# A decoder step on one core: memory K/V projection first, the SSD scan spread among dense tiles, page units and self heads moved behind it

## The chip, the core and the metric

The kernel runs on one core of one Trainium2 chip. The metric is device time in microseconds (us) of one execution. The core has TensorE (matmuls and transposes, results in PSUM), VectorE (DVE in the rows), ScalarE (ACT), GpSimd (POOL) and SyncE (SP, here only an issuer of DMAs). Each engine takes its instructions in the order in which the program lists them, and engines wait for one another by semaphores.

## What is computed

One layer of a hybrid decoder in float32, for a prompt of 256 tokens and 8 samples of 4 tokens with paged caches (288 token columns in all), and a final norm:

```python
proj = rmsnorm(h) @ w_in                       # z, xbc, dt_raw, q, k, v
y_ssd = ssd_branch(z, xbc, dt_raw, ...)        # causal conv, scan in chunks of 128, gate silu(z), norm
y_att = moba_attention(q, k_all, v_all, ...)   # samples: 1024 cached tokens; block top-k, relative bias
h = h + concat([y_ssd, y_att]) @ w_out
h = h + cross_attend(rmsnorm(h), mem_k, mem_v) # 4 heads over 256 memory tokens
h = h + square(relu(rmsnorm(h) @ w_up)) @ w_down
y = rmsnorm(h)
# prompt: mem_k, mem_v = split(rmsnorm(mem) @ w_ca_kv); samples: cached mem_k, mem_v
```

Outputs are also the new k, v, memory k and v, conv states and SSD states (8 heads of 64 for attention, 16 heads of 64 x 128 for the states).

## The kernel before

Activations lie transposed, channels on partitions and the 288 tokens as columns. A dense product is a series of blocks of 256 output columns (a pair of tiles of 128). Its weights (1 MB for 8 k-tiles) stand in one of four slots of `wring`; SyncE loads a block once an earlier one's products are done. A tile is 8 matmuls of 288 columns, each of which the trace shows as two passes, in PSUM bank 0 or 1; VectorE scales the result by `rstd` and writes it out (`tile_out`).

The kinds of tiles are q and k (`qk`, 4 pairs), `v` (2), `z` (4), `x` (6, each followed by the causal conv on VectorE), memory k and v (`m`, 4), `out` (4, with 8 k-tiles from z and 4 from attention), `caq` (2) and `cao` (4). All other results of TensorE (transposes, small products) go through "turns": PSUM banks 2, 3, 6 in rotation, emptied by ScalarE and VectorE alternately (`turn`, `bank`, `leave`).

The cached keys and values of the samples come as 16 *page units* of 2 MB, (K or V, group of four samples, quarter of the cache), eight pages of 256 KB each. `kvring` holds two units. `load_unit` on SyncE waits until the unit two before is used up (`slot_free`: for K its last transposes, for V its products), then loops over eight pages: it reads the page number from `pages` and issues one DMA. A K unit on TensorE is 32 transposes, evicted into `KT_`, and 64 narrow score products (`k_unit`); a V unit is 8 products in two passes (`v_unit`). After the four K units of a group, `own` and `self_bounds` form the scores' maxima and the block choice on VectorE; `probs` transposes the probabilities; `pvend` takes the result after the four V units. The prompt's own attention is eight *self heads* (`head`): scores, bias from DRAM, exp, norm, transposes, values. The units ST, MK and MV (SSD states, memory K and V of the samples) use the same ring with plain DMAs.

The order of everything is written out by hand in `make_plan`; each engine walks through the same list `SEQ` and does its part. Before the change: q/k pairs, with `early` (transposes and norm of the memory prompt, conv history) after the first; K units and pairs (qk, v, m) alternating; V units, self heads and pairs (x, z) alternating; then `ssd`, in one piece: a meeting of all engines, the scan over chunks 0, 1 and the samples' chunk, the state updates; then `out`, `caq`, cross attention, `cao`, MLP.

The SSD part works per chunk: tokens transposed (`xtok`, `btok`), sums of dt, `segments` (exponent matrices of 4 heads, 512 columns), `mix` on VectorE, `outputs`, gate by silu(z), chunk state; for the samples 16 state reads and 16 updates. `sq`, `acc` and the ss products form the sums of squares of a norm: ScalarE squares, GpSimd adds, TensorE sums over partitions, ScalarE takes the root, VectorE the reciprocal (`invert`).

Of the kernel before, what the change touches and what calls it, by code (L numbers as in the profile page):

```python
# [10 lines left out]
ALU = mybir.AluOpType  # L11
# [4 lines left out]
P = 128  # L16
# [91 lines left out]

def make_plan():
    seq = []  # L110

    def pair(kind, n, chunks):
        seq.append(("pair", kind, n, chunks))
# [7 lines left out]
    pair("qk", 0, 1)  # L121
    item("ss", 0)
    item("early")
    pair("qk", 1, 1)
    unit("K", 0, 0)
    pair("qk", 2, 1)
    unit("K", 0, 1)
    pair("qk", 3, 1)
    unit("K", 0, 2)
    pair("v", 0, 1)  # L130
    unit("K", 0, 3)
    item("own", 0)
    pair("v", 1, 1)
    unit("K", 1, 0)
    item("kvtok")
    item("ss", 1)
    pair("m", 0, 1)
    unit("K", 1, 1)
    item("probs", 0)
    pair("m", 1, 1)  # L140
    unit("K", 1, 2)
    pair("m", 2, 1)
    unit("K", 1, 3)
    item("own", 1)
    pair("m", 3, 1)
    item("mtok")
    item("heads_in", "self")
    pair("x", 0, 1)
    unit("V", 0, 0)
    item("head", "self", 0)  # L150
    pair("x", 1, 1)
    unit("V", 0, 1)
    item("head", "self", 1)
    pair("x", 2, 1)
    unit("V", 0, 2)
    item("head", "self", 2)
    pair("x", 3, 1)
    unit("V", 0, 3)
    item("pvend", 0)
    item("probs", 1)  # L160
    item("head", "self", 3)
    pair("x", 4, 1)
    unit("V", 1, 0)
    item("head", "self", 4)
    pair("x", 5, 1)
    item("dt")
    unit("V", 1, 1)
    pair("z", 0, 1)
    item("head", "self", 5)
    pair("z", 1, 1)  # L170
    unit("V", 1, 2)
    item("silu_x")
    item("head", "self", 6)
    pair("z", 2, 1)
    pair("z", 3, 1)
    unit("V", 1, 3)
    item("pvend", 1)
    item("head", "self", 7)
    item("heads_end", "self")
    item("ssd")  # L180
    item("ss", 2)
    for n in range(4):
        pair("out", n, 2)
    pair("caq", 0, 1)
    item("ss", 3)
    pair("caq", 1, 1)
# [15 lines left out]
    for n in range(4):  # L202
        pair("cao", n, 1)
    item("ss", 4)
    return seq


SEQ = make_plan()
BLOCK, TILE, UNIT, TURN = {}, {}, {}, {}
USED = {}  # L210
for s in SEQ:
    if s[0] == "pair":
        for c in range(s[3]):
            if c < s[3] - 1:
                USED[s[1:3] + (c,)] = len(USED)
            BLOCK[s[1:3] + (c,)] = len(BLOCK)
        for h in range(2):
            TILE[s[1:3] + (h,)] = len(TILE)
    elif s[0] == "dt":
        TILE["dt"] = len(TILE)  # L220
    elif s[0] == "unit" and s[1] in ("K", "V"):
        UNIT[s[1:]] = len(UNIT)
    elif s[0] == "ssd":
        for h in range(2):
            UNIT[("ST", h)] = len(UNIT)
    elif s[0] == "unit":
        UNIT[s[1:]] = len(UNIT)
N_BLOCKS, N_TILES, N_USED = len(BLOCK), len(TILE), len(USED)


N_HEADS = {"self": H, "cross": CROSS}
HEAD0 = {"self": 0, "cross": H}


def turn(key):
    TURN[key] = len(TURN)


def plan_turns():
# [3 lines left out]
    for s in SEQ:  # L243
# [3 lines left out]
        elif s[0] == "ss":  # L247
            turn(("ss", s[1]))
        elif s[0] == "early":
            for c in range(DT):  # L250
                turn(("mem", c))
            turn("conv")
        elif s[0] == "kvtok":
            for g in range(3):
                turn(("ktok", g)), turn(("vtok", g))
# [3 lines left out]
        elif s[0] == "own":  # L259
            turn(("own", s[1]))  # L260
# [6 lines left out]
        elif s[0] == "ssd":  # L267
            for i in range(3):
                turn(("cvout", i))
            for q in range(3):  # L270
                turn(("dt", q))
                turn(("xtok", q, 0)), turn(("xtok", q, 1)), turn(("btok", q))
                if q < 2:
                    for hg in range(4):
                        turn(("y", q, hg))
                    turn(("st", q, 0)), turn(("st", q, 1))
                else:
                    for bi in range(GB):
                        for bh in range(G):
                            for g in range(2):  # L280
                                turn(("ss", bi, bh, g))
                    turn(("yd", 0)), turn(("yd", 1))
                    turn("ys")
            turn(("sf", 0)), turn(("sf", 1))
        elif s[0] == "head":
            if s[2]:
                turn(("pv", s[1], s[2] - 1))
            turn(("pt", s[1], s[2]))
        elif s[0] == "heads_end":
            turn(("pv", s[1], N_HEADS[s[1]] - 1))  # L290
# [17 lines left out]
K_TILES = {"qk": 8, "v": 8, "z": 8, "x": 8, "m": 8, "out": 6, "caq": 8, "cao": 4}  # L308


def build(nc, I, O, scratch):
    ctx = ExitStack()
    with ctx:
# [33 lines left out]
        xc = sb("xc", [P, XT, T])  # L347
        qz = sb("qz", [P, 2, PAIRS, NP_])
        kT = sb("kT", [P, PAIRS, T])
        vtok = sb("vtok", [P, 3, 512])  # L350
        attT = sb("attT", [P, 4, T])
        mkv = sb("mkv", [P, 2048])
# [17 lines left out]

        xpad = part(XT * XPAD).rearrange("p (c t) -> p c t", c=XT)
        ssd_at = at[0]
        memw = part(DT * NP_).rearrange("p (c t) -> p c t", c=DT)
        KT_ = part(2 * 1024).rearrange("p (s b t) -> p s b t", s=2, b=GB)
        vT = part(PAIRS * T).rearrange("p (c t) -> p c t", c=PAIRS)
        logit = part(PAST + NS)
        biasS = part(PAST + NS)
        PT = part(9 * P).rearrange("p (c t) -> p c t", c=9)
        osb = part(512)
        ctmp = part(XPAD)  # L380

        stage = xc[:, :, :].rearrange("p c t -> p (c t)")[:, 0:1024].rearrange("p (s t) -> p s t", s=2)
        mstage = big[:, 8192:8192 + 1024].rearrange("p (s t) -> p s t", s=2)

        xin = xc[:, :, :].rearrange("p c t -> p (c t)")[:, 0:3072].rearrange("p (g n) -> p g n", g=3)
        memin = big[:, 8192:8192 + 2048].rearrange("p (g n) -> p g n", g=2)
        cvin = mkv[0:NB * 3, 0:1536]
# [1787 lines left out]
```

## Time and profile before

| | us |
|---|---|
| median of 3 runs (789.83, 789.86, 791.85) | 789.86 |
| the profiled execution, its own time | 791.33 |
| its span in the profile | 789.5 |
| TensorE busy | 709.1 (90%) |
| VectorE busy | 415.8 (53%) |
| ScalarE, GpSimd busy | 142.0, 120.5 |
| DMA moved | 126.2 MB |

The stages, by the time line: start until the first K unit at 59.8; K units, V units and self heads with their pairs until 303.4, where the last V unit starts; the end of the heads until 314; the SSD scan until 420; `out` until 467.45; `caq`, cross attention and `cao` until 549.15; MLP and end until 789.5. A busy TensorE is not always at its peak: its modelled busy time is longer where the granted clock is low. The clock has two levels, 1.2 and 2.4 GHz, and a row gives the mean share of the higher (1.00 is 2.4 GHz, 0.50 is 1.2).

### The profile page before, as it was taken

What the parts mean: (1) busy time and instruction counts of PE and PEld (TensorE: products, weight loads), DVE (VectorE), ACT (ScalarE), POOL (GpSimd) and SP (SyncE); (2) the same over time, 40 slices, a digit from 0 to 9 for tenths busy, and PEclk for the clock granted to TensorE, in tenths of its full rate; (3) what the DMA queues carried; (4) which work ended last, traced back from release to release, by engine and by line L of the source; (5) the groups of instructions that cost most, each with busy time, mean ns of one, the idle gap of its engine ahead of it and who ended that gap; (6) DMA issues with size and microseconds to landing.
All of it is one profiled execution on the core that took longest, in us unless ns stands there. A gap on an engine that the chain in (4) does not pass through costs nothing. (4 is left out here: it accounts for less than half of the span.)

```text
span 789.5 us, 12071 instructions
## 1 busy us (share of the span) xinstructions
PE 709.1 (90%) x4351; PEld 543.4 (69%) x4351; DVE 415.8 (53%) x905; ACT 142.0 (18%) x322; POOL 120.5 (15%) x200
## 2 busy tenths in 40 slices
PE   4879999997999997889879997868999999999993
PEld 2456677785756674543326775537999999999992
DVE  2253244243876821884387222536788887445524
ACT  2131114222101021431111000411211111000002
POOL 3120001003002002200034110003254444000000
PEclk9969999999899999796979998989999999999998
DMA  9563677687779955400006790456354444544401
GB/s 285 135 178 100 207 241 254 224 264 210 220 232 288 294 142 138 137 1 1 1 0 165 235 320 0 147 174 213 108 159 145 145 150 152 186 161 161 160 1 61
DMA packets 102492, 126.18 MB, mean 160 GB/s; under 512 B 6385, under 2 KB 78565, under 8 KB 102440
## 3 DMA queue, kind: packets, MB, share of 16 engines
q1 hardware_dynamic: 99240, 115.08, 46.5%
q0 software_dynamic: 3200, 10.39, 4.6%
q8 instruction: 35, 0.57, 0.3%
q14 instruction: 17, 0.14, 0.1%
HBM read 117.14 MB, written 8.31 MB: 159 GB/s over the span
## 5 line engine op out<-in xcount | busy, mean ns | idle before, releaser
L843 PE MATMUL ps<-hw,wring 128*128 128x288 f32 x576 | 152.3, 426 | 5.7 <-DVE qs L1692 3.7
L843 PEld LDWEIGHTS ps<-hw,wring 128*128 128x128 f32 x576 | 114.5, 200 | 42.4 <-DVE qs L1692 4.1
L1646 DVE COPY tmp<-ps 128x512 f32<-128x512 f32 (+3 forms) x84 | 53.6, 643 | 67.3 <-PE ps L829 61.4
L829 PEld LDWEIGHTS ps<-ident,big 128*128 128x128 f32 x400 | 45.6, 146 | 37.2 <-issue 13.1
L829 PE MATMUL ps<-ident,big 128*128 128x128 f32 x400 | 58.6, 289 | 10.0 <-DVE tmp L1646 6.3
L1441 ACT ACTIVATE tmp<-ps 128x512 f32<-128x512 f32 (+4 forms) x71 | 39.7, 562 | 131.4 <-PE ps L829 111.3
L1239 PE MATMUL ps<-hw,wring 128*128 128x144 f32 x256 | 35.5, 294 | 2.2 <-DVE hw L1649 2.2
L709 POOL TENSOR_TENSOR acc<-acc,sq 128x288 f32<-128x288 f32 (+1 forms) x35 | 27.9, 798 | 52.9 <-ACT sq L1447 50.8
L1239 PEld LDWEIGHTS ps<-hw,wring 128*128 128x128 f32 x256 | 33.7, 196 | 2.7 <-DVE hw L1649 2.7
L1239 PE MATMUL ps<-big,wring 128*128 128x144 f32 x256 | 34.0, 286 | 0.0
L866 PE MATMUL ps<-big,wring 128*128 128x288 f32 x128 | 32.6, 408 | 0.5 <-DVE big L1649 0.5
L1239 PEld LDWEIGHTS ps<-big,wring 128*128 128x128 f32 x256 | 32.4, 190 | 0.0
L866 PEld LDWEIGHTS ps<-big,wring 128*128 128x128 f32 x128 | 24.2, 190 | 7.8 <-DVE big L1649 1.3
L843 PE MATMUL ps<-tmp,wring 128*128 128x256 f32 x128 | 28.5, 381 | 0.0
L924 PE MATMUL ps<-tmp,qs 128*32 128x256 f32 x320 | 25.6, 390 | 2.9 <-ACT tmp L1441 1.6
L758 POOL COPY attT<-ohT 64x16 f32<-64x16 f32 (+1 forms) x24 | 4.6, 194 | 150.6 <-ACT ohT L1441 141.8
L1595 ACT ACTIVATE xc<-ps 128x144 f32<-128x144 f32 x20 | 5.8, 288 | 119.5 <-PE ps L1239 119.5
L843 PEld LDWEIGHTS ps<-tmp,wring 128*128 128x128 f32 x128 | 24.1, 190 | 3.6 <-issue 0.4
L1602 ACT ACTIVATE big<-big 128x288 f32<-128x288 f32 x32 | 13.0, 444 | 74.2 <-DVE big L2113 74.2
L809 POOL TENSOR_TENSOR tmp<-big 128x144 f32<-128x144 f32 x16 | 15.9, 997 | 66.3 <-ACT big L1602 66.3
L829 PE MATMUL ps<-ident,tmp 128*128 128x128 f32 (+1 forms) x94 | 16.1, 304 | 10.0 <-DVE tmp L1772 4.7
L1239 PE MATMUL ps<-tmp 128*128 128x144 f32 x192 | 24.8, 286 | 0.0
(306 smaller groups left out, 1177.1 us busy)
## 6 DMA issues: line engine op xcount, KB each, us to landing
wring<-in_w_in SPq DMA_DIRECT2D x16, 1024.0 KB, 6.9
big<-in_cache_k SPq DMA_DIRECT2D x64, 256.0 KB, 2.7
big<-in_cache_v SPq DMA_DIRECT2D x64, 256.0 KB, 3.5
wring<-in_w_up SPq DMA_DIRECT2D x16, 1024.0 KB, 5.3
wring<-in_w_down SPq DMA_DIRECT2D x16, 1024.0 KB, 5.0
wring<-in_w_out SPq DMA_DIRECT2D x8, 768.0 KB, 8.7
wring<-in_w_ca_kv SPq DMA_DIRECT2D x4, 1024.0 KB, 5.3
big<-in_state_ssm SPq DMA_DIRECT2D x8, 512.0 KB, 6.1
```

Source lines behind the costliest of these rows:

```text
L709: pool.tensor_tensor(a, a, sq[:, m % 2, 0:n], ALU.add).then_inc(acc_done, 1)
L758: copy = pool.tensor_copy(dst, src)
L809: step(pool.tensor_tensor(ff_sums[:, 0, n], a[1], a[0], ALU.subtract))
L829: last = pe.transpose(ps[0:c, bank(key), col:col + r], in_, ident[0:r, 0:r])
L843: last = pe.matmul(ps[:, t % 2, 0:width], w, rhs(c * k_tiles + k), start=(c + k == 0), stop=(c == chunks - 1 and k == k_tiles - 1))
L866: last = pe.matmul(ps[:, t % 2, 0:T], w, z[:, k, :], start=(k == 6), stop=(k == 5))
L924: last = pe.matmul(ps[32 * b:32 * b + 32, bk, lo:lo + 256], qs[:, c, u[1] * GB + b, :], (xKT if cross else KT_)[:, step % 2, b, :], start= ...
L1239: last = pe.matmul(ps[:, bank_, col * HALF:(col + 1) * HALF], w(k), x(k), start=(start and k == 0), stop=(stop and k == 3))
L1441: act.activation(dst, src, ACT.Copy).then_inc(turn_act, 1)
L1595: act.activation(parts[:, u % 2, 0], ps[:, A, 0:HALF], ACT.Copy).then_inc(p1_made, 1)
L1602: act.activation(ff[:, c * T:(c + 1) * T], ff[:, c * T:(c + 1) * T], ACT.Square).then_inc(ff_done, 1)
L1646: dve.tensor_copy(dst, src).then_inc(turn_dve, 1)
```

## The change

`make_plan` is rewritten, and `ssd` is cut into items of its own (`cv`, `tok`, `sums`, `seg`, `stt`, `yd`, `ys`, `upd`, `yo`, `sst`, `zsq`, `state`, `over`). The new order: x and memory transposes, conv history and tables; pairs of x and m in turn; dt; tiles of z, qk and v with the scan's items between single tiles (the samples' chunk first, then chunk 0 and 1); the K units with the last scan items, the k and v transposes (`kvtok`) and `own` between them; V units, each with one self head and one `oz` tile; `oa`, and the rest as before. In detail:

- `out` is split: `oz` (8 k-tiles from z, `tile_out` adds to h) and `oa` (4 k-tiles from attention).
- The ring carries ST first; `load_unit` for unit n+2 stands on SyncE behind unit n; the two first K units are loaded after `seg` 0,1 and 0,3.
- SyncE's first DMAs are in another order: memory prompt, first block, conv state, second block, then the six table loads.
- Turns that only one engine empties are assigned to it; results of the scan (sums, gram, segments, updates, y) and the scores of self heads now go through turns too, instead of banks 4, 5, 0, 1. `gate` reads PSUM directly, `mix` works in place in `E4` (the buffer `M4` is gone), `ssT` has eight buffers instead of four.
- Buffers move: v's transposed copy lies in `attT`; the staging of k is `sq` and `ohT`, so squares wait for k's stores (`kst_out`); page scores (`KT_`, `logit`) lie over the conv and scan buffers, so the engines drain (`over`, `ssd_over`) before K unit 4 and the heads.
- The meeting ahead of the scan is gone.

Cut to its core:

```diff
@@ make_plan
+    item("memt")
+    item("hist")
+    item("tab")
+    pair("x", 0)
+    pair("m", 0)
+    item("ss", "x")
...
     unit("K", 0, 0)
-    pair("qk", 2, 1)
+    item("seg", 1, 2)
+    item("yo", 1, 1)
+    item("kvtok", 0, 2)
...
     unit("V", 0, 0)
-    item("head", "self", 0)
-    pair("x", 1, 1)
+    tile("oz", 0, 0)
+    item("head", "self", 1)
@@ SyncE
-            for s in SEQ:
-                if s[0] == "pair":
-                    for c in range(s[3]):
-                        if BLOCK[s[1:3] + (c,)] >= done:
-                            load_block(s[1:3] + (c,))
-                elif s[0] == "unit":
-                    load_unit(s[1:])
-                elif s[0] == "ssd":
-                    load_unit(("ST", 0))
-                    load_unit(("ST", 1))
+            for s in SEQ:
+                if s[0] == "tile" and s[3] == 1:
+                    g = BLOCK[s[1:3]]
+                    if g + SLOTS < N_BLOCKS:
+                        load_block(g + SLOTS)
+                    if s[1:3] == ("x", 2):
+                        load_unit(0)
+                    elif s[1:3] == ("m", 2):
+                        load_unit(1)
+                elif s == ("seg", 0, 1):
+                    load_unit(2)
+                elif s == ("seg", 0, 3):
+                    load_unit(3)
+                elif s[0] == "unit" and s[1] != "ST" and UNIT[s[1:]] + 2 < len(UNITS):
+                    load_unit(UNIT[s[1:]] + 2)
@@ ScalarE
+                elif s[0] == "zsq":
+                    act.wait_ge(y_used, 4 + s[1] + 1)
+                    act.wait_ge(kst_out[0], 16)
+                    act.wait_ge(kst_out[2], 16)
+                    for c in (2 * s[1], 2 * s[1] + 1):
+                        square("ssd", c, z[:, c, :], T)
```

SyncE among the K units. Before, the load of a unit (the rows from the branch to the compare, run eight times) is followed by a weight block that waits for products:

```order
L594 UNCONDITIONAL_BRANCH [waits turn_ps]
L594 ISA
L595 TENSOR_LOAD pages
L595 ISA x2
L596 ISA
L596 DMA big<-in_cache_k 128x512
L594 REGISTER_ALU
L594 COMPARE_AND_BRANCH
L572 DMA wring<-in_w_in 128x8x256 [waits dense_ps]
L594 UNCONDITIONAL_BRANCH [waits turn_ps]
```

After, one unit's loop stands right behind the other's:

```order
L726 UNCONDITIONAL_BRANCH [waits turn_ps]
L726 ISA
L727 TENSOR_LOAD pages
L727 ISA x2
L728 ISA
L728 DMA big<-in_cache_k 128x512
L726 REGISTER_ALU
L726 COMPARE_AND_BRANCH
L726 UNCONDITIONAL_BRANCH [waits turn_ps]
```

The loop itself is the same; the block between two loops is gone.

TensorE among the K units. Before (`L829` are the transposes, `L924` the scores, `L843` a pair of dense tiles):

```order
L843 MATMUL ps<-hw,wring 128x288 x16
L829 MATMUL ps<-ident,big 128x128 x16
L924 MATMUL ps<-tmp,qs 32x256 x4
L829 MATMUL ps<-ident,big 128x128 x8
L924 MATMUL ps<-tmp,qs 32x256 x4
L829 MATMUL ps<-ident,big 128x128 x8
L924 MATMUL ps<-tmp,qs 32x256 x8
L843 MATMUL ps<-hw,wring 128x288 x16
```

After, from the end of the third K unit to that of the fourth, `own` and the fifth (`L979` are transposes, `L1049` scores, `L1341` is `own`):

```order
L1049 MATMUL ps<-tmp,qs 32x256 x8
L979 MATMUL ps<-ident,tmp 128x128 x8
L979 MATMUL ps<-ident,big 128x128 x16
L1049 MATMUL ps<-tmp,qs 32x256 x4
L979 MATMUL ps<-ident,big 128x128 x8
L1049 MATMUL ps<-tmp,qs 32x256 x4
L979 MATMUL ps<-ident,big 128x128 x8
L1049 MATMUL ps<-tmp,qs 32x256 x8
L1341 MATMUL ps<-kT,qs 32x32 x16
L979 MATMUL ps<-ident,big 128x128 x16
```

No dense tile stands between two K units any more.

ScalarE behind the second K unit, after the change (`L1554` empties a turn, `L1560` squares z for the SSD norm):

```order
L1554 ACTIVATE vtok<-ps 32x512 [waits turn_ps]
L1560 ACTIVATE sq<-big 128x288 [waits kst_out2,acc_done,kst_out0,y_used]
L1560 ACTIVATE sq<-big 128x288 [waits acc_done]
L1560 ACTIVATE sq<-big 128x288 [waits kst_out2,acc_done,kst_out0,y_used]
L1560 ACTIVATE sq<-big 128x288 [waits acc_done]
L1554 ACTIVATE tmp<-ps 128x512 [waits kt_used,turn_ps] x4
```

The squares, which stood at the end of the scan, now stand ahead of the third K unit's evictions (the four `tmp<-ps`) and wait for the stores of k.

SyncE at the start, before and after:

```order
L614 DMA vec_rows<-in_conv_w 48x128
L572 DMA wring<-in_w_in 128x8x256
L616 DMA rb<-in_rel_bias 128x1x8
L617 DMA rb_tab<-in_rel_bias 32x8
L618 DMA step_of<-in_step_of 128x4
L619 DMA big<-in_onehot_s 128x1056
```

```order
L746 DMA vec_rows<-in_conv_w 48x128
L747 DMA tmp<-in_mem_prompt 128x2x1024
L704 DMA wring<-in_w_in 128x8x256
L749 DMA mkv<-in_state_conv 24x1536
L704 DMA wring<-in_w_ca_kv 128x8x256
L751 DMA rb<-in_rel_bias 128x1x8
L752 DMA rb_tab<-in_rel_bias 32x8
```

The tables (rel_bias to mask_p) stand behind 2.2 MB more.

## Rows read from the trace of the kernel before

**Rows 1.** Stages: stretch, its length, busy us (instructions) per engine, clock, DMA share, GB/s

```profile
core 0: us, PE busy (x) PEld busy (x) DVE busy (x) ACT busy (x) POOL busy (x), PEclk, DMA share, GB/s
0.00:789.50 789.50, 709.07 (x4351) 543.41 (x4351) 415.76 (x905) 142.02 (x322) 120.48 (x200) 0.95 0.51 160
59.80:303.40 243.60, 234.97 (x1437) 167.86 (x1435) 116.25 (x257) 47.88 (x106) 16.65 (x35) 0.99 0.71 217
303.40:314.00 10.60, 6.30 (x42) 2.41 (x42) 2.28 (x6) 2.33 (x3) 2.52 (x12) 1.00 0.77 198
314.00:420.00 106.00, 90.30 (x389) 42.88 (x390) 72.06 (x163) 26.96 (x52) 12.87 (x28) 0.84 0.10 32
420.00:467.45 47.45, 46.91 (x193) 36.28 (x192) 18.00 (x38) 5.33 (x10) 13.85 (x17) 1.00 0.84 266
467.45:549.15 81.70, 65.14 (x352) 45.12 (x350) 34.39 (x75) 18.17 (x47) 7.94 (x17) 0.92 0.41 137
549.15:789.50 240.35, 225.57 (x1818) 223.88 (x1818) 152.30 (x326) 26.60 (x67) 51.70 (x68) 0.98 0.41 134
```

**Rows 2.** Time line of SyncE's DMA issues: start us, length us, line, count

```profile
28.98 22.60 SPq L596 DMA_DIRECT2D big<-in_cache_k  x16
...
66.81 10.67 SPq L596 DMA_DIRECT2D big<-in_cache_k  x8
...
251.41 12.62 SPq L596 DMA_DIRECT2D big<-in_cache_v  x8
```

**Rows 3.** The page loop by source line (L595, L596): shortest/median/longest ns

```profile
L595 SPq TENSOR_LOAD <-pages x128: 262/268/688, 28.0 to 277.2; - x128
...
L596 SPq DMA_DIRECT2D big<-in_cache_k x64: 342/348/397, 29.0 to 152.6; - x64
...
DMA to landing us min/median/max: 2.4/2.8/7.0
```

**Rows 4.** Time line of TensorE: start us, length us, line, count of passes

```profile
26.29 10.29 PE L843 MATMUL ps<-hw,wring 128*128 128x288 f32 x32 [2.00 <-DVE wring L2012]
...
89.52 2.04 PE L829 MATMUL ps<-ident,big 128*128 128x128 f32 x16
...
96.09 8.03 PE L843 MATMUL ps<-hw,wring 128*128 128x288 f32 x32
...
129.02 7.07 PE L843 MATMUL ps<-tmp,wring 128*128 128x256 f32 x32
...
208.13 1.92 PE L945 MATMUL ps<-big,tmp 128*32 128x512 f32 x16
...
212.35 7.92 PE L843 MATMUL ps<-hw,wring 128*128 128x288 f32 x32
...
331.43 1.98 PE L1070 MATMUL ps<-tmp 128*128 128x512 f32 x4
...
419.97 2.10 PE L864 MATMUL ps<-attT,wring 128*128 128x288 f32 x8
```

**Rows 5.** Time line of VectorE, in brackets the idle time before and its releaser

```profile
13.27 0.29 DVE L1999 TENSOR_TENSOR wring<-rb,step_of 128x128 f32<-128x128 f32 x1 [13.27 <-DMA wring<-in_mask_p]
...
38.24 1.95 DVE L1726 RECIPROCAL rstd<-rstd 128x288 f32<-128x288 f32 x1 [0.60 <-ACT rstd L1539]
...
111.60 1.23 DVE L1737 TENSOR_REDUCE small<-ps 128x4 f32<-128x1024 f32 x1
...
117.24 0.15 DVE L1754 TENSOR_SCALAR small<-small 128x1 f32<-128x1 f32 x1
...
405.95 13.98 DVE L1942 SCALAR_TENSOR_TENSOR big<-big,dec,ps 128x128 f32<-128x128 f32 x48 [0.58 <-PE ps L1132]
```

**Rows 6.** Time line of GpSimd: the sums of squares

```profile
400.44 6.40 POOL L709 TENSOR_TENSOR acc<-acc,sq 128x288 f32<-128x288 f32 x7
```

**Rows 7.** Stretches of 4 us: TensorE busy, clock, DMA share, GB/s

```profile
8.00:12.00 4.00, 2.79 (x10) 1.00 1.08 366
192.00:196.00 4.00, 0.48 (x8) 0.84 0.39 89
196.00:200.00 4.00, 3.62 (x11) 0.50 0.84 209
```

**Rows 8.** DMA issues between 120 and 200 us: KB, us to landing

```profile
out_sample_k<-xc POOLq DMA_DIRECT2D x1, 64.0 KB, 3.1
```

More of the change, by code:

```diff
@@ new lines, in make_plan @@
+    pair("x", 5)
+    item("dt")
+    tile("z", 0, 0)
+    item("dt_series")
+    tile("z", 0, 1)
+    item("dt_rates")
+    tile("z", 1, 0)
+    item("silu_x")
+    tile("z", 1, 1)
+    tile("z", 2, 0)
+    item("cv")
+    item("tok", 2)
+    tile("z", 2, 1)
+    item("sums", 2)
+    tile("z", 3, 0)
+    item("seg", 2, 0)
+    item("stt")
+    tile("z", 3, 1)
+    item("silu_z")
+    item("yd")
+    item("upd", 0, 2)
+    tile("qk", 0, 0)
+    item("ys")
+    item("upd", 2, 6)
+    tile("qk", 0, 1)
@@ new lines, in make_plan @@
+    item("upd", 6, 10)
+    item("tok", 0)
+    tile("qk", 1, 0)
+    item("upd", 10, 14)
+    tile("qk", 1, 1)
+    item("upd", 14, 16)
+    item("sums", 0)
+    tile("qk", 2, 0)
+    item("seg", 0, 0)
+    tile("qk", 2, 1)
+    item("seg", 0, 1)
+    item("yo", 0, 0)
+    tile("qk", 3, 0)
+    item("seg", 0, 2)
+    item("yo", 0, 1)
+    tile("qk", 3, 1)
+    item("seg", 0, 3)
+    item("yo", 0, 2)
+    tile("v", 0, 0)
+    item("yo", 0, 3)
+    item("sst", 0)
+    item("tok", 1)
+    tile("v", 0, 1)
@@ L129, in make_plan @@
+    item("sums", 1)
+    tile("v", 1, 0)
+    item("seg", 1, 0)
+    tile("v", 1, 1)
+    item("seg", 1, 1)
+    item("yo", 1, 0)
+    unit("K", 0, 0)
+    item("seg", 1, 2)
+    item("yo", 1, 1)
+    item("kvtok", 0, 2)
+    item("seg", 1, 3)
+    item("yo", 1, 2)
+    unit("K", 0, 1)
+    item("yo", 1, 3)
+    item("sst", 1)
+    item("kvtok", 2, 3)
+    item("zsq", 0)
+    item("zsq", 1)
     unit("K", 0, 2)
-    pair("v", 0, 1)
+    item("zsq", 2)
+    item("zsq", 3)
+    item("state")
+    item("over")
@@ L236, in turn @@
+TURN_KEYS, EVICTOR, PLACE_OF = [], {}, {}
+def turn(key, engine=None):
+    if engine is None:
+        engine = "act" if sum(1 for k in TURN_KEYS if k in FREELY) % 2 == 0 else "dve"
+        FREELY.add(key)
     TURN[key] = len(TURN)
+    EVICTOR[key] = engine
+    PLACE_OF[key] = sum(1 for k in TURN_KEYS if EVICTOR[k] == engine) + 1
+    TURN_KEYS.append(key)
+FREELY = set()
 def plan_turns():
@@ L259, in plan_turns @@
         elif s[0] == "own":
[L260 removed]
+            turn(s)
         elif s[0] == "probs":
@@ L1529, in _ @@
+            leave("vec")
+            for c in range(DT):
+                leave(("x", c))
+                turned(act, ("x", c))
+                square("x", c, h3[:, c, :], T)
             for s in SEQ:
```

1435 lines of the change are left out of this document (735 added, 700 removed).

## Prediction, made before the changed kernel was run

> **What bounds the kernel now.** The table of stages comes first [rows 1]. TensorE is busy 709 of the 789.5 us, so the whole kernel can give back some 80 us of idle time, plus what the low clock costs (granted clock 0.95 over the span). The last stage (240.35 us, MLP and end) is full, and its code stays. The SSD scan (314 to 420) has little else beside it: 106 us, clock 0.84, DVE 72 us busy, DMA 0.10. That stage is what hiding the scan could shorten. Between 59.8 and 303.4 the reader should see a TensorE that hardly waits (235 us busy of 243.6) although sixteen units of 2 MB of cache pages, 32 MB, are used there: between two units stands a pair of dense tiles.
>
> The second view is the queue of SyncE [rows 2]. The loop that loads a unit issues eight DMAs, and takes 10.67 to 12.62 us for them (the shortest and the longest of 14; the first two units, with nothing to wait for, take 22.60 together). The rows by line say why [rows 3]: one turn of the loop is a load of the page number (0.27 us), its register work, and 0.35 us for the DMA, one after the other, some 1.35 us. The data are there 2.8 us after the issue. So SyncE delivers one unit per 11.3 us (22.60 / 2) however idle the rest is. Before, TensorE comes back for a unit every 14.4 us (a unit of 6.57 us and a pair of 8.03) [rows 4], and this limit is not seen. The question for the change is what stands between the units now.
>
> **Term 1, until the first key unit: 287 us.** The six table loads now stand behind the memory prompt, the conv state and two weight blocks. DVE's first instruction waits for them and the x evictions queue behind it [rows 5]. Between them lie 1.0 + 0.14 + 1.0 MB more, which at 366 GB/s [rows 7] are 5.9 us: the evictions of x start at 19.2 instead of 13.3 and end near 25. The eight memory tiles then follow at the pace of GpSimd's sums of squares, 0.91 each [rows 6], 7.5 us; conv history, table products and their VectorE copies follow, 8 us by what lies between 18.5, where x ended, and the first dense tile at 26.29 [rows 4]: the first dense tile starts near 41.
> Dense work from there: 16 pairs x 8.03 and 4 memory pairs x 7.07 [rows 4] are 156.8; dt 3.8, transposes and sums 3.2; together 163.8. Scan work on TensorE: some 90 passes of 512 columns before that unit at 0.45 (four took 1.98 with their tail) [rows 4], 40; 64 state transposes at 0.13 (16 in 2.04) [rows 4], 8; the other transposes, the y products and the small ones, 17; together 65. Stalls: x1 needs a bank that x0 holds until the reciprocal is there, about 4.4; the first pair and the one after that wait run slow, as the first does now (10.29 instead of 8.03) [rows 4], 5; handoffs of the scan, each behind a tile of 4 us, bounded by 0 and 20, taken as 8, because VectorE's 16 updates (48 of their 64 operations in 13.98, so 1.17 each) [rows 5] and its tile evictions nearly fill the time there. 41 + 163.8 + 65 + 4.4 + 5 + 8 = 287, bounds 275 and 300.
>
> **Term 2, key units back to back: 110 us from the start of the first to the landing of the first value unit.** Two slots hold units, so the load of unit n+2 waits for the last transposes of unit n. At SyncE's pace alone: 5.6 us of the first unit, seven loads x 11.3, landing 2.8: 87.5. On top comes time in which SyncE waits for a slot, because what stood under dense tiles now stands between units:
> - scan pieces and token transposes of k, v between units 1 and 2: unit 2 is consumed some 7 us after SyncE has ended its load (5 to 8);
> - the squares behind unit 2 wait for the stores of k, since the staging buffer is now the squares' buffer: store landing 3.1 [rows 8], then four squares at 0.91 [rows 6], all ahead of unit 3's evictions on ScalarE: 5 to 12;
> - four more squares, two state operations and the drain of both evicting engines ahead of unit 4: 3 to 6;
> - self_bounds (6.1 us of VectorE, 111.60 to 117.39) [rows 5], followed at once by unit 5; before, a pair of tiles stood there: 2 to 6;
> - the root and reciprocal (1.95) [rows 5] before unit 6: 0 to 3.
> Together 15 to 35; I take 22, nearer to the low end since SyncE's queue soaks up part of each: 110. Nothing makes this less than 87.5.
> TensorE is idle some 4 us in each 11.3. After an idle stretch of that length the granted clock fell to 0.50, that is 1.2 GHz, for 4 us or more (192 to 200) [rows 7]. Units then take longer than 6.57, which the 11.3 mostly hides. The Trainium skill (TensorE: Matmul & The Clock Gate, Why this matters for your kernels) asks for no idle gaps beyond some 3 us between bursts; by that rule alone the order of before, which has none there, is the better one.
>
> **Term 3, value units: 80 us** to the landing of the eighth: seven loads x 11.3 and the small loads of w_out in the same queue (3 x 0.4). TensorE needs for a unit 1.92, for a tile half a pair, 4.0, and for a head 2.4 (210.0 to 212.35) [rows 4], 8.3 us, so it waits for SyncE each time. The bias transfers that VectorE waits for in the heads have 11 us each.
>
> **Term 4, the rest: 348 us.** After the last unit: its products, result, one tile, last head, the copies of the samples' heads, 10.3 (the like took 10.6, from 303.4) [rows 1]. The eight w_out tiles keep only their attention part, 8 passes in 2.10 with the tail [rows 4], 15.6 instead of 47.45 for all. Then 81.70 and 240.35 as before [rows 1].
>
> **Sum:** 287 + 110 + 80 + 348 = 825. I take 822, since the first two handoffs of term 2 partly overlap. The profiled execution took 791.33 for a span of 789.5; its time lies 1.5 above the median of 789.86, its span 0.4 below it, so the sum can stand as the median within half a us: **822**, 4.1% slower. The scan is under dense tiles then, and costs about its own TensorE time. But the dense tiles that stood between the units are used up by it, and the unit stretch shrinks only from 243.6 to 190, because SyncE sets its length.
>
> **Rivals.**
> 1. Key units at SyncE's pace alone, the handoffs hidden: 287 + 87.5 + 80 + 348 = 802.5. For it: each handoff is shorter than a load. Against it: with two slots a delay of one unit delays the next load but one.
> 2. Issue is no limit, and the kernel gets faster. Place: SyncE's page loop; price: if a unit cost only the time of its bytes (2.1 MB at 366 GB/s, 5.7 us), TensorE would set the pace: K 8 x 6.57 + 14 for the pieces between = 67, V 7 x 8.3 = 58, so 287 + 67 + 58 + 348 = 760, or 748 with term 1 at its low bound. It decides as soon as a turn of the loop takes under 0.8 us, an eighth of a K unit. Against it: no loop is under 10.67 [rows 2].
> The Trainium skill (DMA: Bandwidth & Descriptors, Issuing engines are not separate DMA queues) says that the sequencer's time to start a DMA is usually small against the DMA. Here one turn costs 1.35 us against 0.7 for 256 KB at 366 GB/s; the trace disagrees for this loop, because the page number is fetched in it. By the page's rule the time would be that of this rival.
> 3. The change doesn't do what it says, the scan is not hidden: chains between VectorE and ScalarE make TensorE wait at every second item. Term 1 grows by 15 to 25 and the sum to 840 to 850. Against it: VectorE has the 72 us of the scan stage [rows 1] and some 20 of tiles and dt in the 150 us there.
>
> **How the numbers follow.** Forecast 0.58, with 806 to 838 (term 1 at 275 to 300, term 2 at 102 to 122); rival 1: 0.18, 794 to 806; rival 2: 0.10, 745 to 785; rival 3: 0.10, 838 to 855; between rivals 2 and 1, around no change: 0.04. The range 794 to 842 holds the first two and a third of rival 3, 0.8. A measurement of this kernel can tell 0.3%, 2.4 us, from no change. Faster than that: rival 2 and 0.01 of the last case, 0.11; within it: 0.03; slower: 0.86.
>
> **What would show it.** SyncE's queue after the first key unit: loops of 10.7 to 12.6 us with almost no gap among the value units, gaps of 5 to 10 us after the second and third key unit. TensorE: four us of idle before each value unit, released by in_cache_v, and a clock well under 1.00 among the key units. First dense tile at 41, not 26; first key unit at 275 to 300; first value unit 100 to 115 later; last value unit 80 after that. The scan stretch with DVE above 0.6 and TensorE above 0.9. The forecast is wrong if the page loops take less than 9 us, or if the first key unit starts before 265.

## Result and profile after

The changed kernel takes **826.90 us** (median of 4 runs, 823.53 to 828.22) against 790.16 for the kernel before in the same comparison: ratio 1.0454, 95% interval 1.0419 to 1.0489. The forecast was 822 in a range of 794 to 842. The profiled execution took 827.45, with a span of 825.5; the sums below are sums of this span.

The stages of the changed kernel, in one table, so that they can be set against the terms of the prediction (columns: stretch, its length, busy us (instructions) per engine, clock, DMA share, GB/s):

```profile
0.00:43.35 43.35, 19.36 (x61) 9.50 (x61) 15.30 (x36) 10.71 (x26) 14.97 (x25) 1.00 0.51 150
43.35:276.96 233.61, 226.09 (x995) 161.60 (x995) 120.86 (x287) 32.42 (x47) 15.08 (x34) 0.94 0.51 152
276.96:304.00 27.04, 24.96 (x214) 15.31 (x212) 14.82 (x30) 8.96 (x15) 2.18 (x4) 1.00 0.50 158
304.00:345.00 41.00, 21.77 (x183) 15.31 (x182) 20.31 (x38) 12.22 (x30) 12.03 (x16) 0.78 0.57 159
345.00:392.19 47.19, 32.79 (x303) 21.08 (x302) 23.86 (x46) 16.68 (x36) 3.02 (x5) 0.90 0.59 162
392.19:475.42 83.23, 67.82 (x322) 37.31 (x322) 26.85 (x58) 10.91 (x37) 5.82 (x16) 0.90 0.72 201
475.42:825.50 350.08, 316.19 (x2280) 286.68 (x2280) 193.14 (x416) 50.30 (x123) 66.36 (x99) 0.96 0.43 140
```

The first key unit starts at 276.96, the first value unit's products at 392.19, the eighth's at 475.42. The stretch that replaces the scan [rows 1] is full now: TensorE is busy 226.1 of 233.6 us. In all TensorE is busy 709.0 us as before, but the span has 116.5 us in which it is idle, 36.1 more than the 80.4 before. Of the 116.5, 75.1 lie in three places: the start (24.0 of 43.35), the key units (35.7 of 115.2) and the value units (15.4 of 83.2). Of the rest, 33.9 lie behind the eighth value unit and 7.5 in the stretch with the scan.

| stretch | forecast | measured |
|---|---|---|
| start until the first dense tile (part of the next row) | 41 | 43.35 |
| start until the first key unit | 287 (275 to 300) | 277.0 |
| key units until the first value unit | 110 | 115.2 |
| value units until the eighth | 80 | 83.2 |
| the rest | 348 | 350.1 |
| sum of the last four | 825 | 825.5 |

In the key units, TensorE's time line gives three single stops of 5 to 8 us (columns: start us, length us, line, count; in brackets the idle time before and its releaser):

```profile
311.37 1.12 PE L979 MATMUL ps<-ident,big 128*128 128x128 f32 x4 [5.74 <-DVE tmp L1775]
...
324.73 1.97 PE L979 MATMUL ps<-ident,tmp 128*128 128x128 f32 x8 [5.54 <-DVE tmp L2051]
326.49 3.62 PE L979 MATMUL ps<-ident,big 128*128 128x128 f32 x16
...
344.76 1.12 PE L979 MATMUL ps<-ident,big 128*128 128x128 f32 x4 [7.48 <-ACT tmp L1554]
```

The first stands inside the third unit. TensorE makes three turns of transposes, then needs the bank of the first, which nobody has emptied. By the kernel's rotation this bank is VectorE's to empty, and the row names VectorE's copy (L1775). The time lines of ScalarE and then of VectorE (same columns) say why it is late: ScalarE's squares wait for the store of the samples' k out of `sq`, VectorE scales each part of z (L1778) behind its square, and only then come the evictions (`tmp<-ps`) of both:

```profile
304.24 0.59 ACT L1554 ACTIVATE vtok<-ps 32x512 f32<-32x512 f32 x1 [0.28 <-PE ps L985]
307.59 0.78 ACT L1560 ACTIVATE sq<-big 128x288 f32<-128x288 f32 x2 [2.76 <-DMA out_sample_k<-sq]
308.64 0.44 ACT L1560 ACTIVATE sq<-big 128x288 f32<-128x288 f32 x1 [0.27 <-POOL acc L846]
309.65 0.44 ACT L1560 ACTIVATE sq<-big 128x288 f32<-128x288 f32 x1 [0.57 <-POOL acc L849]
310.00 0.58 ACT L1554 ACTIVATE tmp<-ps 128x512 f32<-128x512 f32 x1
```

```profile
308.07 0.89 DVE L1778 TENSOR_SCALAR big<-big,vec 128x288 f32<-128x288 f32 x2 [3.58 <-ACT sq L1560]
309.11 0.67 DVE L1778 TENSOR_SCALAR big<-big,vec 128x288 f32<-128x288 f32 x1
310.12 0.59 DVE L1778 TENSOR_SCALAR big<-big,vec 128x288 f32<-128x288 f32 x1 [0.34 <-ACT sq L1560]
310.64 1.27 DVE L1775 COPY tmp<-ps 128x512 f32<-128x512 f32 x2
```

The second stop is the second half of the squares with the state's two operations on VectorE: here TensorE waits for the state that it is to transpose, not for a bank. The third is `self_bounds` on VectorE (336.03 to 341.81) with five exponentials behind it on ScalarE, which hold the evictions of the fifth unit. A fourth, of 3.75 us, is the root and reciprocal. From 304 to 345, where the first three stand, the clock is 0.78.

The waits of TensorE in the value units, in one view (columns: engine, line, releaser, us in total, times, longest):

```profile
PE ps L1070 <- DMA big<-in_cache_v: 20.7, 6, 6.6
PE ps L979 <- DVE tmp L1896: 1.2, 1, 1.2
```

The longest of the six, 6.56 us, ends at 392.19 and so still belongs to the key units; the others make up 14.1 of the 15.4 us in which TensorE is idle among the value units.

SyncE's time line (start, length, count) shows why TensorE waits: 32 page DMAs stand in a row with no wait for anybody between them (the last row):

```profile
241.08 10.86 SPq L728 DMA_DIRECT2D big<-in_cache_k  x8
...
284.35 90.13 SPq L728 DMA_DIRECT2D big<-in_cache_k  x48
375.60 46.70 SPq L728 DMA_DIRECT2D big<-in_cache_v  x32
```

Those 32 DMAs lie 46.35 / 31 = 1.495 us apart, which is 12.0 us a unit.

### The profile page after: what moved, and what is told of

Same layout as the page of the kernel before. It is cut to its first block and busy times, and to the rows that moved or that the text cites. A ratio compares the mean times of both kernels' runs of the same rounds, so it can differ in the third digit from the quotient of the medians.

```text
span 825.5 us, 12067 instructions
## 1 busy us (share of the span) xinstructions
PE 709.0 (86%) x4351; PEld 546.8 (66%) x4351; DVE 415.2 (50%) x908; ACT 142.2 (17%) x312; POOL 119.5 (14%) x199
## 5 line engine op out<-in xcount | busy, mean ns | idle before, releaser
L1020 PE MATMUL ps<-hw,wring 128*128 128x288 f32 x576 | 158.3, 435 | 11.9 <-DVE tmp L1807 5.0
L1020 PEld LDWEIGHTS ps<-hw,wring 128*128 128x128 f32 x576 | 116.5, 205 | 52.9 <-issue 5.8
L979 PE MATMUL ps<-ident,big 128*128 128x128 f32 x384 | 57.5, 300 | 26.4 <-DVE tmp L1775 14.0
L1775 DVE COPY tmp<-ps 128x512 f32<-128x512 f32 (+3 forms) x76 | 49.8, 663 | 54.5 <-PE ps L979 52.4
L979 PEld LDWEIGHTS ps<-ident,big 128*128 128x128 f32 x384 | 46.5, 153 | 44.3 <-DVE tmp L1775 15.9
L1554 ACT ACTIVATE tmp<-ps 128x512 f32<-128x512 f32 (+3 forms) x74 | 41.8, 568 | 160.9 <-PE ps L979 76.7
L1070 PE MATMUL ps<-big,tmp 128*32 128x512 f32 x160 | 24.0, 727 | 20.7 <-DMA big<-in_cache_v 20.7
L1020 PE MATMUL ps<-attT,wring 128*128 128x288 f32 x128 | 33.0, 421 | 2.7 <-POOL attT L905 1.9
L979 PE MATMUL ps<-ident,tmp 128*128 128x128 f32 (+1 forms) x110 | 22.7, 343 | 13.7 <-DVE tmp L1896 5.7
L1020 PEld LDWEIGHTS ps<-attT,wring 128*128 128x128 f32 x128 | 25.1, 198 | 10.4 <-issue 2.1
L1049 PE MATMUL ps<-tmp,qs 128*32 128x256 f32 x320 | 28.6, 431 | 2.5 <-ACT tmp L1554 1.3
L979 PEld LDWEIGHTS ps<-ident,tmp 128*128 128x128 f32 (+1 forms) x110 | 14.8, 168 | 24.0 <-DVE tmp L1896 8.1
L1822 DVE TENSOR_TENSOR tmp<-ps,rstd 128x288 f32<-128x288 f32 x8 | 3.7, 457 | 47.3 <-PE ps L1020 47.3
```

The lines of the kernel that those rows point to most:

```text
L979: last = pe.transpose(ps[0:c, bank(key), col:col + r], in_, ident[0:r, 0:r])
L1020: last = pe.matmul(ps[:, BANK[key], 0:width], w, rhs, start=(k == 0), stop=(k == K_TILES[kind] - 1))
L1049: last = pe.matmul(ps[32 * b:32 * b + 32, bk, lo:lo + 256], qs[:, c, u[1] * GB + b, :], KT_[:, step % 2, b, :], start=(c == 0), stop=(c == 3),
L1070: last = pe.matmul(ps[32 * b:32 * b + 32, 7, :], (xPT if cross else PT)[:, col, 32 * b:32 * b + 32], src[:, b, t, :], start=(first and t = ...
L1554: act.activation(dst, src, ACT.Copy).then_inc(turn_act, 1)
L1775: dve.tensor_copy(dst, src).then_inc(turn_dve, 1)
```

## Experiments

All comparisons are with the kernel before on the same chip. It took 789.26 in the group of e1 to e4, 787.71 in that of e5 to e7 and 788.66 in that of e8 to e10, so that savings between groups are known to a microsecond or two only.

| run | median us | ratio to before, interval |
|---|---|---|
| changed kernel | 826.90 | 1.0454 (1.0419 to 1.0489) |
| e1 quick pages | 804.62 | 1.0186 (1.0160 to 1.0211) |
| e2 before, quick pages | 783.62 | 0.9930 (0.9905 to 0.9954) |
| e3 squares later | 818.54 | 1.0361 (1.0340 to 1.0382) |
| e4 v tiles among the key units | 812.88 | 1.0296 (1.0257 to 1.0334) |
| e5 = e1 and e3 | 790.85 | 1.0038 (1.0000 to 1.0075) |
| e6 tables first | 817.67 | 1.0405 (1.0310 to 1.0499) |
| e7 v tiles, quick pages, tables | 786.81 | 0.9995 (0.9961 to 1.0029) |
| e8 handoffs covered, quick pages, tables | 767.29 | 0.9731 (0.9692 to 0.9771) |
| e9 as e8, page loop as changed | 796.36 | 1.0102 (1.0053 to 1.0152) |
| e10 fixed pages (a single run) | 804.46 | |

### e1 and e2: the page loop made cheap

```diff
-                    with sp.Fori(0, 8) as i:
-                        page = sp.value_load(pages[0:1, ds(i + first, 1)], ...)
-                        sp.dma_start(big[:, ds(i * 512 + (n % 2) * 4096, 512)], cache[ds(page, 1)]...)
+                    for j in range(0, 8, 4):
+                        _, got = nc.values_load_multi_w_load_instructions(pages[0:1, first + j:first + j + 4], ...)
+                        for i, page in enumerate(got):
+                            at_ = (i + j) * 512 + (n % 2) * 4096
+                            sp.dma_start(big[:, at_:at_ + 512], cache[ds(page, 1)]...)
```

> The changed kernel with one edit: SyncE reads four page numbers in one load and then issues four page DMAs, twice per unit, with no loop; order, waits and data are the same. Theory S (SyncE's page loop sets the pace of the unit stretch, 12 us a unit in the value units): a unit is issued in 5 to 7 us instead of 10.8; the value stretch falls from 83 to 58 to 64 (TensorE needs 8.3 a unit), the key stretch from 115 to 85 to 98 since the waits for TensorE and the evictions stay; together 770 to 795. Rival H (handoffs of the key stretch and the landing of the data set the pace, the loop only fills the waiting): the two stretches stay within 5 us each, 818 to 827. Rival V (the loop limits the value units alone): 803 to 808.

> The kernel before with the same edit of SyncE. Theory S: its loop was hidden under a unit and a pair of dense tiles (14.4 us), so 786 to 791, no difference of 0.5%. Rival (the loop cost something there too, in the value units with 12.3 us a unit): 775 to 783.

e1: 804.62, 22.3 less, where rival V stands and not theory S. SyncE's time line of e1:

```profile
240.74 5.44 SPq L732 DMA_DIRECT2D big<-in_cache_k  x8
...
283.40 88.26 SPq L732 DMA_DIRECT2D big<-in_cache_k  x48
```

A unit is issued in 5.44 us instead of 10.86, yet the 48 page DMAs of the key units still stretch over 88.26 us against 90.13. Between units SyncE waits for TensorE now. The stages of e1 say the same: the key units take 112.89 (115.23 in the changed kernel), the value units 65.48 (83.23).

```profile
275.45:388.34 112.89, 83.01 (x697) 53.88 (x696) 52.97 (x94) 35.86 (x73) 15.26 (x22) 0.85 0.50 159
388.34:453.82 65.48, 61.40 (x323) 35.88 (x322) 31.79 (x74) 12.66 (x43) 7.71 (x20) 0.97 0.88 272
```

So the loop set the pace of the value units (17.7 us), and not of the key units. There TensorE had waited 9.2 us for pages (2.6 for the eighth unit, 6.6 for the first value unit), and this is gone, but most of it comes back elsewhere: its waits for the two evicting engines grow from 26.3 to 29.8 us, and its own work from 79.5 to 83.0 at a clock of 0.85 instead of 0.88.

e2: 783.62, 5.6 us or 0.7% less than before, while no difference was expected; it lies just above the rival's range too, and its cause is not the rival's. In the traces 5.8 us lie at one place, between the first two value units (190.55 to 208.13 before, 190.82 to 202.59 in e2); the two profiled executions differ by 7.6, and what else they differ by lies mostly behind the heads, in code with no page in it. TensorE there waits for the first self head, which waits for its bias from DRAM. The rows are VectorE's and TensorE's of before, and then those of e2:

```profile
192.03 0.69 DVE L1963 SCALAR_TENSOR_TENSOR tmp<-ps,tmp 128x512 f32<-128x512 f32 x1 [10.73 <-DMA tmp<-bias_rows]
...
196.38 1.11 PE L829 MATMUL ps<-ident,tmp 128*128 128x128 f32 x4 [3.91 <-DVE tmp L1972]
...
199.00 9.20 PE L843 MATMUL ps<-hw,wring 128*128 128x288 f32 x32
```

```profile
189.02 0.69 DVE L1967 SCALAR_TENSOR_TENSOR tmp<-ps,tmp 128x512 f32<-128x512 f32 x1 [7.46 <-DMA tmp<-bias_rows]
...
193.38 0.66 PE L833 MATMUL ps<-ident,tmp 128*128 128x128 f32 x4 [0.64 <-DVE tmp L1976]
...
194.74 7.92 PE L847 MATMUL ps<-hw,wring 128*128 128x288 f32 x32
```

TensorE's wait shrinks by 3.3 us, and what follows runs at full clock: the pair takes 7.92 instead of 9.20. GpSimd issues the bias loads at the same time in both (182.89 and 183.16), behind four stores of the memory k and v; these land after 3.3 and 3.4 us in e2 instead of 5.6 and 7.6. That the pages, issued sooner, leave the DMA engines free for them fits these numbers. So does another reading: the weight block of 1 MB behind the pages is issued at 181.24 before, among the stores (180.72 to 182.36), and already at 176.76 in e2. No run separates the two.

### e3 and e5: the squares moved, with the slow and the quick loop

```diff
     unit("K", 0, 1)
...
-    item("zsq", 0)
-    item("zsq", 1)
     unit("K", 0, 2)
-    item("zsq", 2)
-    item("zsq", 3)
     item("state")
     item("over")
+    item("zsq", 0)
     unit("K", 0, 3)
     item("own", 0)
+    item("zsq", 1)
     unit("K", 1, 0)
-    item("ss", "ssd")
+    item("zsq", 2)
     unit("K", 1, 1)
+    item("zsq", 3)
     item("probs", 0)
     unit("K", 1, 2)
+    item("ss", "ssd")
```

> The changed kernel with the slow page loop, and the eight squares of z spread behind the third to sixth key unit instead of behind the second and third, the state store and the drain ahead of the fourth; the root of the SSD norm behind the seventh. Theory S with handoffs on top: the squares no longer wait for the stores of k ahead of the third unit's evictions, SyncE's waits for slots (18 us in the key stretch) fall to 8 to 13, the time by 5 to 10: 817 to 822. Rival (the handoff only moves, since each unit's evictions and self_bounds still stand between units): 825 to 828.

> The changed kernel with both edits, four page numbers per load and the squares spread among the third to sixth key unit. Theory P (in the key stretch two limits lie close together: the handoffs, which held it at 113 with quick pages, and SyncE's loop, which took over as soon as the squares were moved: TensorE then waited 15.7 us there for pages): with both taken away these 15.7 us go as well, so more than the sum of the single edits (22 and 8): 782 to 791. Rival A (the two savings just add): 794 to 798. Rival B (self_bounds and the other handoffs left hold it at once): 798 to 803.

e3: 818.54, 8.4 less. The first stop is gone, the second is down to 1.3 us, and at once TensorE waits for pages in the key units. First the waits of the changed kernel between the first key and the first value unit, then those of e3 (same columns as above):

```profile
PE ps L979 <- DVE tmp L1775: 10.6, 5, 5.7
PE ps L979 <- ACT tmp L1554: 7.5, 1, 7.5
PE ps L979 <- DVE tmp L2051: 5.5, 1, 5.5
PE ps L979 <- DMA big<-in_cache_k: 2.6, 1, 2.6
```

```profile
PE ps L979 <- DMA big<-in_cache_k: 13.2, 3, 8.0
PE ps L979 <- ACT tmp L1554: 6.6, 2, 4.7
PE ps L979 <- DVE tmp L2078: 2.5, 2, 1.7
PE ps L979 <- DVE tmp L2051: 1.3, 1, 1.3
```

e5, both edits: 790.85, within theory P's range. The single savings add to 30.7, which would be 796.2; measured are 36.1. The 5 us between them are not clear of the noise of the four medians, but the traces show 4 of them in the key units: this stretch is 115.2 us in the changed kernel, 112.9 in e1, 106.2 in e3 and 99.8 in e5, so the edits give 2.3 and 9.1 alone and 15.4 together. The two limits overlap there, as theory P says, though by 4 to 5 us and not by 15: of the 13.2 us for pages 3.1 remain, and the wait behind `self_bounds` grows from 4.7 to 8.3.

### e4: the v tiles among the key units again

```diff
-    tile("v", 0, 0)
     item("yo", 0, 3)
...
     unit("K", 0, 0)
     item("seg", 1, 2)
     item("yo", 1, 1)
-    item("kvtok", 0, 2)
+    tile("v", 0, 0)
...
     unit("K", 0, 1)
     item("yo", 1, 3)
+    tile("v", 0, 1)
...
     unit("K", 0, 2)
     item("state")
+    tile("v", 1, 0)
     item("over")
     unit("K", 0, 3)
     item("own", 0)
+    tile("v", 1, 1)
     unit("K", 1, 0)
+    item("kvtok", 0, 2)
+    item("kvtok", 2, 3)
```

Behind the sixth unit follow the first four squares, behind the seventh the other four and the sum of the SSD norm.

> The changed kernel with the slow page loop and a part of the change undone: the four tiles of v (4.04 us each) stand between the key units again, with the transposes of k and v behind the fifth unit and the squares behind the sixth and seventh. Theory S: TensorE idles 36 us in the key stretch, so the tiles are absorbed there; the part ahead of the first key unit gets 10 to 16 shorter, the key stretch grows by at most 5: 812 to 820. Rival (TensorE and the evictions set the pace of the key units): the stretch grows by the 16 us that the part ahead loses, 825 to 832.

812.88, 14.0 less. The first key unit starts at 263.05 instead of 276.96, and the key units take 113.17 although 16 us of tiles now stand in them. This order also moves the squares, as e3 does (to other places), so the 14 us are not the tiles' alone. Set against e3, 5.7 us are left: the first key unit starts 13.0 us earlier (263.05 against 276.07), and the key units are 7.0 longer (113.17 against 106.16). So the idle time of the key units takes in a good half of the 16 us of dense work, and TensorE's waits for key pages fall from 13.2 us to 0.8.

### e6: the tables first

```diff
+            sp.dma_start(rb4[:, :], ...)
...
+            sp.dma_start(mask_p, I["mask_p"])
             sp.dma_start(memin, I["mem_prompt"]...)
             load_block(0)
             sp.dma_start(cvin, I["state_conv"])
             load_block(1)
-            sp.dma_start(rb4[:, :], ...)
...
-            sp.dma_start(mask_p, I["mask_p"])
```

> The changed kernel with SyncE's six table loads ahead of the memory prompt, the conv state and the two weight blocks again, all else as changed. Theory of the prediction: VectorE's first instruction and the x evictions behind it wait for the tables, so the first dense tile comes 5 to 7 us earlier and so does the end: 819 to 823. Rival (the start is then held by the memory prompt or the first weight block instead, which land later): 825 to 829.

817.67, 9.2 less, more than expected. One of its four executions took 825.12, hence the wide interval; the trace says where the gain lies. VectorE's first instruction in the changed kernel and in e6:

```profile
21.24 0.29 DVE L2115 TENSOR_TENSOR wring<-rb,step_of 128x128 f32<-128x128 f32 x1 [21.24 <-DMA wring<-in_mask_p]
```

```profile
10.79 0.29 DVE L2115 TENSOR_TENSOR wring<-rb,step_of 128x128 f32<-128x128 f32 x1 [10.79 <-DMA wring<-in_mask_p]
```

The first dense tile moves from 43.35 to 32.16, by 11.2 us where 5 to 7 were expected for the bytes ahead of the tables. The first table load alone holds SyncE for 3.90 us behind the large loads, against 0.72 in e6, and `mask_p` is issued at 14.65 instead of 7.46. In the kernel before, one 1 MB block stands ahead of the tables and the instruction starts at 13.27 [rows 5].

### e10: what a turn of the loop costs

```diff
-                        page = sp.value_load(pages[0:1, ds(i + first, 1)], ...)
+                        page = i + first % 32
```

> The changed kernel with the loop kept but the page number computed from the loop's counter instead of loaded, so the samples attend to other pages than asked for. If the fetch of the page number is the price of a turn, a turn takes 0.5 to 0.8 us instead of 1.50 and a unit is issued in 4 to 6.4 us; the time is within 3 of the run with quick pages alone, 802 to 807. If the loop's own branch and register work is the price, a turn stays above 1.1 us and the time above 812.

```profile
237.59 6.11 SPq L728 DMA_DIRECT2D big<-in_cache_k  x8
```

Here the samples attend to other pages than asked for, so this run says only what the fetch costs. A turn takes 0.80 to 0.90 us in most units (1.06 in one), against 1.50: a little over the 0.5 to 0.8 expected, and far from the 1.1 of the other reading. So the fetch of the number is worth some 0.6 to 0.7 us of a turn, although its own row shows only 0.27. With it come 0.16 of register work and a bounds check of 0.02, a part of the register work ahead of the DMA (0.08, where e10 has 0.04 or none), and time between these instructions. In e1 four numbers come with one load, whose row (below) reads 0.30 us. Its DMAs follow 0.52 apart within a group of four, and 1.9 from one group to the next, where the load and the register work of the next four stand:

```profile
L727 SPq TENSOR_LOAD <-pages x32: 294/298/979, 238.1 to 444.5; - x32
```

The time, 804.46, is that of e1 (804.62), as expected.

### e7, e8, e9: the handoffs put under dense tiles

e7 has the order of e4 with quick pages, tables first, and the root of the SSD norm behind the eighth key unit. e8 changes this much more:

```diff
     unit("K", 0, 2)
     item("state")
-    tile("v", 1, 0)
     item("over")
+    item("bias")
     unit("K", 0, 3)
     item("own", 0)
+    tile("v", 1, 0)
     tile("v", 1, 1)
     unit("K", 1, 0)
```

At `bias` GpSimd issues the bias loads of the first two heads, which it did at `heads_in` until then.

> The changed kernel with quick pages, tables first and the four v tiles among the key units, squares behind the sixth and seventh, the root behind the eighth. Theory P: 812.9 of the run with v tiles, less 18 to 20 for the value units, less 5 for the 5 us that TensorE still waited for pages in the key stretch there, less 5 for the start: 782 to 787, under the kernel before. Rival (the savings overlap, the key stretch has other limits): 790 to 798.

> The changed kernel with quick pages, tables first, all four v tiles among the key units but two of them right behind own, so that self_bounds and its exponentials run under them, and the first two bias loads of the heads issued behind the drain instead of behind the squares. Theory C (what is left of the key stretch are single handoffs, each with its price in the trace of the run with v tiles, quick pages and tables: 3.7 at self_bounds, 8.8 at the head bounds that waited for the bias): 786.8 less 3.7 and less 5 to 8.8: 774 to 779, faster than the kernel before. Rival (the two waits are replaced by the next ones, such as the pages of the eighth unit): 782 to 788.

> The same order with the page loop of the changed kernel. The value units then go at the loop's pace again. Theory C: 18 to 22 more for the value units and 3 to 8 more in the key stretch, 796 to 806, slower than the kernel before. Rival (with the handoffs covered the loop costs only the value units what it did, 18): 792 to 796.

e7: 786.81, within the expected range and with no measurable difference to before. It has a stop that was mine: the squares, which GpSimd adds, stood ahead of the bias loads in GpSimd's queue, so the head bounds and with them TensorE waited 8.8 us in the eighth unit. The row is TensorE's:

```profile
354.56 1.12 PE L983 MATMUL ps<-ident,big 128*128 128x128 f32 x4 [8.82 <-DVE tmp L2082]
```

e8: 767.29, **2.7% faster than the kernel before** and, by the ratios to before, 6.9% faster than the changed one. That is below the ranges of both theory C and its rival, and below e2 (783.62). Its waits of TensorE over the key units have no entry above 3.5 us; its stages:

```profile
252.19:355.45 103.26, 91.23 (x762) 60.28 (x760) 52.74 (x97) 35.39 (x73) 14.12 (x22) 0.95 0.60 188
355.45:419.48 64.03, 59.81 (x323) 34.59 (x322) 33.46 (x75) 12.90 (x44) 7.83 (x20) 1.00 0.91 280
```

The gain over e7 was larger than the 12.5 us of the two stops. In the traces the key stretch got 13.4 shorter (116.6 in e7, from 253.38 to 369.99) and starts 1.2 earlier, 14.5 together. Of the 13.4, 10.7 are idle time of TensorE and 2.7 are work done in less time, at a clock of 0.95 instead of 0.90. The rest of the 19.5 between the medians lies within the spread of the runs (784.67 to 792.27 for e7, 765.58 to 771.57 for e8).

e9, the same order with the page loop of the changed kernel: 796.36, so the loop costs 29 us here by the medians and 23.5 by the spans of the profiled runs (793.3 and 769.8). By the traces 21.8 of them are the value units (85.79 against 64.03) and only 0.9 the key units (104.13 against 103.26), where I had expected 3 to 8, so here the rival was nearer. In the key units the tiles cover the loop. What the medians show beyond the traces is in no trace.

## Why the prediction was right, and where its reasons were wrong

The time lies in the range and the two things named as the cause, SyncE's loop and the handoffs, are real. That 825 meets the span of 825.5 is luck: term 1 is 10 us too high, and terms 2 to 4 together are 10.5 too low. The 3 us taken off for an overlap of handoffs, which gave 822, only took the forecast further away. Its upper bound was also added wrongly: terms at 300 and 122 give 850, not 838.

**Term 1** (277.0 for 287). The start was right: the tables behind 2.2 MB more move the first dense tile to 43.35 (41 forecast), and e6 shows that this order costs 9 us, the one part of the loss that buys nothing. VectorE's first instruction came at 21.24 for 19.2. From the first tile on I asked for 246 and it took 233.6. The wait for the reciprocal was right (4.96 us measured, 4.4 forecast), the slow pairs too (9.72 and 10.93 for two of 8.03). The handoffs of the scan were mis-sized: taken as 8, but from 76 us to the first key unit all of TensorE's waits together are under 3 us. The work itself was also set too high: 163.8 + 65 + 5 = 233.8 against 226.1 busy. The scan does disappear under dense tiles; rival 3 is refuted. One sign failed: VectorE is busy 120.9 of the 233.6 us, 0.52 and not above 0.6.

**Term 2** (115.2 for 110): the sum was near, the build-up was wrong. I started from SyncE's pace as a floor, 87.5, and put 22 of waits for slots on it. (With the true price of a turn, 1.50 us, that would have been 92 and 114, and SyncE's own waits for slots do come to 18; the sum agrees, and still names the wrong cause.) e1 takes the pace away, and the stretch loses 2.3 us. What makes up the stretch is TensorE's own work, 79.5 busy, its stops behind the evicting engines, 26.3, and at the end 9.2 for pages. The list of handoffs was right by place: squares behind the stores (5.7 measured, 5 to 12), second squares and drain (5.5, 3 to 6), `self_bounds` (7.5, expected 2 to 6: I had left out the exponentials that ScalarE makes ahead of its evictions; its work on VectorE is 5.8 us by the two rows quoted, not 6.1), root and reciprocal (3.75, 0 to 3); the scan pieces behind the first unit cost TensorE nothing (24.96 busy of 27.04). The step that failed is "SyncE's queue soaks up part of each". It is the other way about: the stops stand on TensorE's path and most of the loop disappears in them, until the stops are shortened (e3, e5). The numbers that could have told me were there: the 67 of rival 2 for TensorE's work and the 22 of handoffs are 89, no less than SyncE's 87.5. In the trace the key units take 115.2 / 8 = 14.4 us each, against SyncE's 12.0.

**Term 3** (83.2 for 80): the mechanism was right, as e1 shows (65.5 without it). The size of a unit was off, because I divided 22.60 by two: that row runs from the first DMA to the end of the sixteenth and leaves out the rest of the last turn. By intervals it is 22.25 / 15 = 1.483 a turn and 11.9 a unit, which would have given 84.

**Term 4** (350.1 for 348) was right.

**Two rules and the trace.** The Trainium skill's rule against gaps (TensorE: Matmul & The Clock Gate, Why this matters for your kernels) agrees with this trace: the granted clock is 0.78 where TensorE idles 19 of 41 us, and transposes of 16 take 3.6 us at 326.49, behind a stop of 5.5, instead of 2.0. Over the whole kernel this cost nothing more than before, since TensorE is busy 709.0 us in both: the scan stage ran at 0.84 before [rows 1]. The remark of the Trainium skill on the sequencer's small share (DMA: Bandwidth & Descriptors, Issuing engines are not separate DMA queues) does not hold for this loop, which takes 1.50 us for 256 KB.

**The rivals.** Still, rival 2 is refuted. The page DMAs of e1 stand 0.73 us apart (5.09 / 7), under the 0.8 from which it was to decide, and the time is 804.6 and not 760. The rival had priced the key units as TensorE's work and 14 us of pieces, without the stops. Only e8, where these are covered too and the tables come first, lies in the rival's range of 745 to 785, and by another sum. Rival 1 (802.5) lost since its handoffs are not hidden.

**What the loss is made of.** The page loop without cover costs 22.3 us (e1), but quick pages also gain 5.6 in the order before (e2), so 17 of the difference between the two kernels are the loop's. The tables at the start cost 9. Of the stops between the key units, moving the squares recovers 8 with the slow loop (e3) and 14 with the quick one (e5 against e1). Together that is 34 to 40 for a net loss of 37, so these runs do not say whether the hidden scan pays anything as the change stands. With the causes put right it does: e8 gives 767.29 (ratio 0.9731), against 783.62 (0.9930) for the order before with quick pages. Whether the order before could gain more from repairs of its own was not tried.

## What to carry to other kernels

Dense tiles between short, chained pieces of work are cover, for the queue that feeds them and for the engines that evict; before such tiles are moved elsewhere to hide something larger, list per unit everything that ran under them (issue time, handoffs, bounds) and leave one tile at each. When two limits lie close together, one experiment that removes one of them proves little: remove both, and each alone. And take the price of a repeated step from the distance of its starts, not from the length of a grouped row.

## What the runs showed of the hardware that I had not expected

- A load of one number into a register of SyncE takes 0.27 us and a load of four 0.30, and what comes with a fetched number (register work, a check) costs a turn more than the fetch itself. Eight pages are issued in 10.86 us with one load each, in 6.11 without loads, in 5.44 with two loads of four and no loop.
- Large transfers on SyncE's queue and the landing of another queue's go together: with the pages and the weight block behind them issued sooner (e2), the stores of memory k and v on GpSimd's queue landed after 3.3 and 3.4 us (medians) instead of 5.6 and 7.6. Which of the two transfers matters is open.
- An issue itself can be held up: the load of the 4 KB table `rb` took SyncE 3.90 us behind 3.2 MB of loads that it had just issued, and 0.72 us ahead of them (e6).
- With three banks in rotation, an eviction that is late by more than two turns stops TensorE, though the unit's data are there: the stops of 5.7 and 7.5 us come from VectorE or ScalarE doing something else first.
